# Moving the split of the up weights, the sums of squares and the last gated sums in a two-block float32 kernel

## The reference

```python
h = rmsnorm(x, g_mix)
z = h @ w_in
...
a = silu(layernorm(a, ln_a_g, ln_a_b));  y_a = a @ w_a_out
x = x + (g_a * y_a + g_b * y_b) @ w_o
h = rmsnorm(x, g_ffn)
u = h @ w_up                                          # 1024 x 5632
f_gate = causal_dwconv(u[..., :D_FF], conv_f_w) + conv_f_b
f = gelu(f_gate) * u[..., D_FF:]                      # D_FF = 2816
x = x + f @ w_down
pg = sigmoid(rmsnorm(x, g_ple) @ w_ple_gate)
x = x + pg * (p @ w_ple)
return rmsnorm(x, g_final)
```

## Time and profile before

| | us |
|---|---|
| median of 3 runs | 1533.56 (1532.98 to 1535.13) |
| the profiled execution, its own time | 1529.72 |
| its span in the profile | 1528.0 |
| outside the span | 1.7 |
| TensorE matmuls busy | 1283.3 |
| VectorE busy | 1094.1 |
| ScalarE busy | 607.9 |

### The profile page before, as it was taken

One profiled execution on the slowest core, in us unless ns is written; L12 is line 12 of the kernel. 1 busy time (PEld: TensorE's weight loads), 2 busy tenths in 40 slices (PEclk: granted clock), 3 DMA queues, 4 the chain that ended last, 5 costly groups with the idle time before them and its releaser, 6 DMA issues. The chain is left out here.

```text
span 1528.0 us, 19779 instructions
## 1 busy us (share of the span) xinstructions
PE 1283.3 (84%) x7076; PEld 965.1 (63%) x7076; DVE 1094.1 (72%) x2196; ACT 607.9 (40%) x1247; POOL 280.9 (18%) x278
## 2 busy tenths in 40 slices
PE   2879899998887987777777787777699989899997
PEld 2879899998884333322222233233299979899996
DVE  7469847555767867777777777775589977777656
ACT  2335546453623433333332233333453254444444
POOL 0000000000053553334434434332000000000000
PEclk7789999999998999999999999999799999999998
DMA  7475653243497999999999999999635434444450
GB/s 313 155 253 216 248 193 111 84 163 131 151 385 290 421 420 422 420 422 421 421 420 421 421 421 422 421 422 424 256 111 187 154 135 166 166 166 148 172 205 28
DMA packets 55374, 416.58 MB, mean 273 GB/s; under 512 B 6000, under 2 KB 7664, under 8 KB 8832
## 3 DMA queue, kind: packets, MB, share of 16 engines
q0 software_dynamic: 36864, 268.45, 42.4%
q1 hardware_dynamic: 18112, 146.71, 26.1%
q10 hardware_dynamic: 320, 0.36, 0.1%
HBM read 414.45 MB, written 1.05 MB: 272 GB/s over the span
## 5 line engine op out<-in xcount | busy, mean ns | idle before, releaser
L957 PE MATMUL ps<-arena 128*128 128x512 f32 x512 | 241.0, 617 | 81.3 <-ACT arena L1360 81.3
L957 PE MATMUL ps<-ring,arena 128*128 128x512 f32 x448 | 220.1, 640 | 44.6 <-ACT arena L1360 44.4
L957 PEld LDWEIGHTS ps<-arena 128*128 128x128 f32 x512 | 95.4, 195 | 225.4 <-ACT arena L1360 119.1
L1978 DVE CUSTOM_DVE_ANT_0 arena<-arena 128x1024 f32<-128x1024 f32 x128 | 151.7, 1224 | 114.5 <-DMA arena<-in_experts,rowid 112.5
L636 PE MATMUL ps<-h_hi,w_hi 128*128 128x256 f32 x704 | 202.8, 288 | 15.5 <-DVE arena L2096 10.2
L560 POOL DMA_INDIRECT arena<-in_experts,rowid x128 | 132.0, 1031 | 400.7 <-DVE rowid L1952 222.1
L638 PE MATMUL ps<-h_lo,w_hi 128*128 128x256 f32 x704 | 199.0, 283 | 0.0
L637 PE MATMUL ps<-h_hi,w_lo 128*128 128x256 f32 x704 | 198.9, 283 | 0.0
L957 PEld LDWEIGHTS ps<-ring,arena 128*128 128x128 f32 x448 | 87.7, 204 | 175.7 <-issue 96.2
L1353 ACT ACTIVATE arena<-arena 128x2 f32<-128x2 f32 x128 | 26.0, 203 | 398.7 <-DVE arena L1978 398.6
L1617 DVE TENSOR_TENSOR w_lo<-arena,w_hi 128x4096 fp32r<-128x4096 f32 (+1 forms) x32 | 130.9, 4091 | 56.4 <-ACT w_hi L1099 56.2
(11 more groups left out here) (334 smaller groups left out, 2512.9 us busy)
## 6 DMA issues: line engine op xcount, KB each, us to landing
ring<-in_early_w SPq DMA_DIRECT2D x47, 1024.0 KB, 5.0
arena<-in_up_w SPq DMA_DIRECT2D x11, 2048.0 KB, 8.0
arena<-in_z_w SPq DMA_DIRECT2D x9, 2048.0 KB, 8.8
arena<-in_ada_w SPq DMA_DIRECT2D x16, 1024.0 KB, 5.0
arena<-in_down_w SPq DMA_DIRECT2D x8, 1408.0 KB, 6.6
ring<-in_ada_w SPq DMA_DIRECT2D x8, 1024.0 KB, 7.5
arena<-in_o_w SPq DMA_DIRECT2D x2, 2048.0 KB, 7.8
arena<-in_pg_w SPq DMA_DIRECT2D x2, 2048.0 KB, 8.2
```

Of the source, the lines that this page charges most:

```text
L957: mm = pe.matmul(BK[4 + 2 * t + b], diag[:, j, :], rows[j][:, D + b * 512:D + (b + 1) * 512], start=first and j == 0, stop=last and j == E ...
L1978: v.tensor_tensor_reduce(out=u, in0=u, in1=h2tok[:, t, :], scale=1.0, scalar=0.0, op0=ALU.mult, op1=ALU.add, accum_out=dots[:, even, j:j + ...
```

## The change

Six edits, on ScalarE's and VectorE's lists only:

1. Up stage, ScalarE: the `part()` ahead of the loop goes, and in each iteration `part()` stands before the two gelus, not behind them. It now makes chunk i+2 in iteration i.
2. Up stage, VectorE: `rest()` is left out of iteration 0, and one is added behind the last `values`. In iteration i it now makes chunk i+1.
3. The eight squares before the up stage and before the `pg` stage are folded by `gather_squares`: three additions into the first two blocks, the first (up) or the first two (`pg`) of them ahead of the last two residual sums.
4. The first reciprocal of the start norm (L2089) moves to behind the layer norm's mean (L2176).
5. Tail: the gated sums of blocks 5, 6 and 7 follow directly on their own block, the additions of squares 5 and 6 stand behind the last gated sum, and ScalarE loads the table for the root after the last block's `ready_out`, not before it.
6. `ready_out` writes the square before the scaled copy.

```diff
@@ ScalarE @@
             late_root("nff")
             act.preload_act_table(ACT.Gelu_apprx_tanh)
-            part()
...
                 if i:
                     part_f(2 * i - 2)
                     part_f(2 * i - 1)
+                part()
                 gelu_f(2 * i)
                 gelu_f(2 * i + 1)
-                part()
...
             def ready_out(k):
                 act.wait_ge(S("x5"), k + 1)
+                act.activation(sq[:, k, :], xT[:, k, :], ACT.Square).then_inc(S("nl_sq"), 1)
                 act.activation(x5g[:, k, :], xT[:, k, :], ACT.Copy, scale=col("g_final_2", k)).then_inc(S("x5g"), 1)
-                act.activation(sq[:, k, :], xT[:, k, :], ACT.Square).then_inc(S("nl_sq"), 1)
             for b in range(KD):
                 gate_p(b)
-                if b:
+                if b and b < 6:
                     ready_out(b - 1)
+                if b >= 5:
+                    ready_out(b)
             act.preload_act_table(ACT.Sqrt)
-            ready_out(KD - 1)
@@ VectorE @@
+            def gather_squares(tag, ready, i):
+                v.wait_ge(S(ready), 2 * i + 2)
+                ins = v.tensor_tensor(sq[:, 0:2, :], sq[:, 0:2, :], sq[:, 2 * i:2 * i + 2, :], ALU.add)
+                if i == 3:
+                    ins.then_inc(S(tag + "_added"), 1)
+                else:
+                    link(ins)
...
-            v.wait_ge(S("nm_root"), 1)
-            v.reciprocal(stat[:, 0, :], ln1)
             v.wait_ge(S("nm_root"), 2)
...
             link(ins, "ln_mean")
+            link(v.reciprocal(stat[:, 0, :], ln1))
             for k in range(KD):
                 ins = stt(xT[:, k, :], xT[:, k, :], col("final_norm_g", k), stat[:, 0, :])
...
                 if k == 5:
                     rest()
+                    gather_squares("nff", "nff_sq", 1)
             lo_of_x("up", 7, col("g_ffn_2", 7))
+            gather_squares("nff", "nff_sq", 2)
+            gather_squares("nff", "nff_sq", 3)
             link(v.memset(upad[:, :, 0:2], 0.0))
-            add_squares("nff", sq, "nff_sq", 0)
             rest()
             inverse(1)
...
                 if i:
                     values(i - 1)
-                rest()
-                if i:
+                    rest()
                     rest_of_f(2 * i - 2)
                     rest_of_f(2 * i - 1)
                 gates(i)
             values(FB // 2 - 1)
+            rest()
             rest_of_f(FB - 2)
...
+            gather_squares("np", "np_sq", 1)
+            gather_squares("np", "np_sq", 2)
             for k in (6, 7):
                 residual("down", k)
             for k in (6, 7):
                 lo_of_x("pg", k, col("g_ple_2", k))
-            add_squares("np", sq, "np_sq", 0)
+            gather_squares("np", "np_sq", 3)
...
                 scaled(("pg", b), gelu2[:, b % 4, :])
-                if b:
+                if b and b < 6:
                     gated_ple(b - 1)
-                if b >= 3:
+                if b >= 5:
+                    gated_ple(b)
+                if 3 <= b < 7:
                     add_to_first("nl", b - 2)
-            add_to_first("nl", 6)
-            gated_ple(7)
+            for k in (5, 6):
+                add_to_first("nl", k)
```

## The result

The changed kernel takes 1516.41 us, median of 4 runs (1513.92 to 1519.21), beside 1533.38 us of the kernel before in 4 runs (1532.98 to 1535.13): ratio 0.9888, 95% interval 0.9868 to 0.9908, 17.0 us faster. The forecast was 1520.1 with a range from 1517.5 to 1525.0.

The account below looks back on a forecast made before the run. TensorE, 84% busy, lost 1.26 us per up-stage iteration waiting for VectorE. Terms -13.35 + 1.06 + 0.17 - 1.37 = -13.5 took the profiled 1529.72 to 1516.2; plus 3.84 to the runs' median, forecast 1520.1 us, range 1517.5 to 1525.0.

Parts of the forecast that it names:

- Up stage: Up stage: VectorE's iteration falls to about 10.65 us, TensorE becomes the bound with period 11.30; -13.35 us.
- 1.7 us of work lost to the clock: Up stage's start: behind TensorE's 3.41 us stop the granted clock is 0.52 for 3.5 us, losing 1.7 us of work.
- Slower, by loads ahead of the gelus: Up stage rival: ScalarE's load waits slow the loop, from a landing of 17.4 us; at 20 us 1541.4; chance 0.02.
- they don't wait: Up stage, ScalarE: gelus behind the high half aren't delayed; their waiting behind a load would show the prediction wrong.
- by as much an iteration: Up stage: the low half's slack before TensorE wants it is 0.65 us at first and grows 0.65 each iteration.
- t + 0.5: Up stage: high half ready 0.5 us after t, when the low half ends and TensorE begins chunk i+1; needed at t + 6.2.
- VectorE still the bound: Up stage rival: VectorE's work and growing gelu wait keep the period, only 5.4 us gained, 1528.2 us; chance 0.05.
- part of the gain stays out: Up stage rival: TensorE keeps waiting 0.6 us in nine iterations, gain 8.1 us, 1525.5 us; chance 0.13.
- First reciprocal: Layer norm: moved reciprocal lengthens the chain, its start norm lead lost in a wait; +1.06 us, bounds 0 and 1.8.
- Squares before `pg`: Before the `pg` sum: two additions moved ahead of the residuals use no idle time; +0.17 us, bounds -0.2 and +0.6.
- Tail: Tail: last copy no longer behind gated sum, additions and table load; -1.37 us, bounds -1.5 and 0.
- No drain behind the table load: Tail: no drain after the table load; rival of a second 1.28 us there gives 1520.5 us, 1 chance in 50.

Follow-up runs that it names:

- e7: Kernel before with 14 small unread matmuls filling TensorE's stop at the up stage's start: 1533.08 us, ratio 1.0004.
- e5: Kernel before with only ScalarE's half of the up stage's edits (high half ahead of the gelus): 1552.96 us, ratio 1.0127.
- e13: Kernel before, unchanged, profiled again for the pace of its z stage: single run of 1530.68 us.
- e16: Kernel before with both up stage edits alone, plus seven small unread matmuls in TensorE's stop before the first o matmul: 1518.59 us, one run.
- e2: Changed kernel, unchanged, run and profiled again: 1518.22 us, ratio 0.9908.
- e4: Changed kernel with the moved reciprocal ahead of the wait for the layer norm's sum and two additions of `pg` squares moved into the down stage: 1514.54 us, ratio 0.989.
- e12: Changed kernel, unchanged, run once more for its scatter: 1515.7 us, ratio 0.9897.
- e8: Changed kernel with the first reciprocal put back at the start norm: 1518.36 us, ratio 0.9902.

## Why the prediction was right or wrong

**Up stage: right.** Forecast -13.35, measured -13.73; TensorE became the bound, its restarts vanished, VectorE's 10.61 us iteration was forecast as 10.65, the clock stayed full, and the stop of 0.2 us left at chunk 2 did not come. The prediction also speaks of 1.7 us of work lost to the clock and prices two rivals with it; e7 shows that this was no part of the stage's length. The forecast itself took the stage's whole length against TensorE's work, so it held.

**Slower, by loads ahead of the gelus: the rival did not come, but its sign did.** The landing stayed at 8.1 us, far from the 17.4 that the rival needed. The prediction said of the gelus "they don't wait", named their waiting behind a load as a sign of being wrong, and let the slack grow "by as much an iteration" to the end. ScalarE waited up to 5.22 us for loads in front of the gelus, three iterations had late gelus, and the slack stopped growing at 3.1 to 3.9 us. By the prediction's own times this was to be seen: the high half is there at t + 0.5, tied to TensorE by the load, and the gelus are wanted at t + 3.7 less VectorE's lead, so they wait once the lead is above 3.2 us. The sign was too strict: a lead that has run out of loads costs nothing while TensorE never stops. *VectorE still the bound* and *part of the gain stays out* are refuted by a timeline without stops. e5 shows where the danger was: in one half without the other, which costs 18 us.

**First reciprocal: the step that failed.** "Inserted 1.75 + 0.05, less 0.78: +1.06" was right for its place (+1.04), but the term for the stages ahead of up came out as -0.63, 1.69 less. The step took the clock and TensorE's pace there to be those of the profiled execution. That one is of the kind that loses no clock there: it ran its z stage at the slow pace and had a stop of only 0.68 us before the layer norm's sum, as three of the 12 other profiles with the old place did. The remaining nine had the stop of 2.37 us, and all lost something: in four (e13 to e16) the clock fell at the sum, in six behind the stop before the o matmuls (e13 at both). Of the five with the new place two show it at the sum (e2, e4) and one, e4, before the o matmuls. So with the old place it took on average 0.9 us more up to the first up matmul than in the profile that the step was worked out from (177.7 against 176.84), and with the new place it took 176.9. The bound of 0 below was too tight. The lead was also not wholly swallowed in the z stage: the wait before the fourth chunk's low half took 0.97 us, against 0.21 to 0.24 with the old place at the same pace, not the 1.75 of the forecast. From TensorE's first matmul of line 978 to that of the layer norm's sum it took 111.98 in the five profiles with the reciprocal moved and 112.18 to 112.23 in those with the old place at the same pace, so 0.2 us was kept. Why the clock falls at the one stop and not at the other stays open.

**Squares before `pg`: right.** +0.17 forecast, +0.06 measured, within a scatter of 0.4.

**Tail: mis-sized.** -1.37 forecast, -1.77 measured. The order is worth what the rows said; left out was that the clock had already fallen when the old order came to its last sums, a thing visible in the profile before (clock 0.67 above), and that the new order is mostly through them by then. The changed kernel's own profile shows only -1.13 here, because its clock fell at the `pg` sum instead (L1005, 1.87 us for four matmuls, 1.02 in e12).

**No drain behind the table load: right.** The root started 0.29 us after the load had ended, so nothing like 1.38 us stood behind it. The drain that the Trainium skill gives (ScalarE: Activation LUTs, "What ACT_TABLE_LOAD costs") would by an estimate put it near 1512.8 (1511.46 and 1.38); no run here shows that drain. The gelus at 1382.51 stood behind the waiting high half until it was made. This agrees again with the Trainium skill (PSUM — Partial Sum Buffer, "Engine vs sequencer instructions"), which calls ScalarE's queue strictly FIFO.

**The range.** By stages the change is worth -16.1 and not -13.5: -0.38 up, -1.69 ahead of up, -0.11 `pg`, -0.43 in the tail and at the end. The other 0.9 of the first 17.0 is taken to be scatter: over all runs the difference is 15.9. "Runs differ by 1 us either way" was read off three runs; the changed kernel's runs have a standard deviation of 2.4, and the first z matmul alone comes anywhere from 1107.5 to 1113.3 in kernels that are the same up to there. A range for this sum should have reached down to about 1515.

## What to carry to other kernels

When the slower of two coupled engines waits in each iteration for work that its partner could have done earlier, move the producer and the consumer together, and check each half alone on paper: one half can be worth nearly everything, the other can be a loss. A clock loss behind a stop is a term of its own only where TensorE sets the pace; in the one stage that was tested with another engine in front it was already in the waits. Small edits near the critical path should be priced with the clock's fall on both sides, and from more than one profile, since a stop that is removed or shifted may be worth more than the instruction moved.

## What was not expected of the hardware

- The same matmul stream starts one every 0.1178 us or one every 0.1222 us at a granted clock of 1.00, and the pace changes between executions of one kernel and inside a stage. In e8 it changed in the up stage without any stop, and as TensorE was the bound there, the stage took 129.19 instead of 125.47. What sets it stays open. The runs of the changed kernel scatter somewhat more (standard deviation 2.4 us in 14 runs against 1.8 in 62); that this comes from the pace is a guess, as its three profiles all have an up stage of 125.5 us.
- The granted clock falls behind some stops of 1.9 to 2.4 us and not behind others of the same length at the same place (L702 above, 1.99 to 3.23 us behind 2.37). What decides it was not settled.
- One execution in the whole study took 4509.07 us, at a mean clock of 1.00.
